# Four edits to the opening of a three-block transformer kernel: statistics by pairs of row tiles, half-block loads, one modulation block summed partly by TensorE, two weight tiles split by GpSimd

## The reference, cut to what matters

```python
c_act = jax.nn.silu(c)
mod = c_act @ ada_w[l] + ada_b[l]
shift, scale, gate = jnp.split(mod[:, None, :], 3, axis=-1)
u = _rmsnorm(h, norm_g[l]) * (1.0 + scale) + shift
proj = u @ w_in[l]                  # 1024 x 1024 times 1024 x 7168
```

## Time and profile before

| | |
|---|---|
| median of 3 runs | 2764.53 us |
| span of the profiled execution | 2763.9 us (the median is 0.6 us above it) |
| TensorE busy | 2689.4 us, 97% of the span |
| VectorE, ScalarE, GpSimd busy | 2086.6, 1069.2, 477.0 us |
| the chain that ended last, by engine | TensorE 80%, VectorE 14%, issue 2% |
| opening, until the last matmul's end | 66.9 us |
| next block's first matmul | starts at 67.8 us |

### The profile page before, as it was taken

The page is one execution under the profiler, slowest core; times in us unless marked ns, Lnnn a source line. Parts: engine busy times, 40 slices in busy tenths (PEclk is TensorE's granted clock), DMA queues, the critical chain, the costliest instruction groups (busy, mean ns, idle before and its releaser), DMA issues.

```text
span 2763.9 us, 33573 instructions
## 1 busy us (share of the span) xinstructions
PE 2689.4 (97%) x13192; PEld 2199.6 (80%) x13192; DVE 2086.6 (75%) x2796; ACT 1069.2 (39%) x1599; POOL 477.0 (17%) x254
## 2 busy tenths in 40 slices
PE   6999999999999999999999999999999999999998
PEld 5888888888888878778875678888887888888887
DVE  6999998873724663369998886688186988887978
ACT  5111112243413332245537751365232554555332
POOL 0000000000100002001210001354211656655000
PEclk8999999999999999999999999999999999999999
DMA  5312222224325452011101032100132222225431
GB/s 223 116 63 69 94 97 61 84 92 142 99 107 175 136 176 90 31 62 39 47 30 36 32 123 96 46 31 23 62 115 80 96 77 89 87 77 188 170 99 61
DMA packets 97710, 250.18 MB, mean 91 GB/s; under 512 B 7361, under 2 KB 34369, under 8 KB 96018
## 3 DMA queue, kind: packets, MB, share of 16 engines
q1 hardware_dynamic: 93010, 231.49, 24.4%
q10 hardware_dynamic: 4288, 15.73, 1.5%
q0 software_dynamic: 256, 0.82, 0.1%
HBM read 202.92 MB, written 45.09 MB: 90 GB/s over the span
## 4 chain that ended last, share of the span: by engine, by line
PE 80%; DVE 14%; issue 2%; ACT 1%; DMA 1%; DVEq 0%; ACTq 0%
PE pair L370 16%; PE pair L372 16%; PE pair L371 16%; PE pair L3657 7%; PE pair L3242 5%; PE pair L3244 5%; PE pair L3245 5%; DVE counted L1942 3%; PE pair L2593 2%; DVE reached L1993 1%; PE pair L2156 1%; DVE top_i L1999 1%; PE pair L1754 1%; PE pair L2172 1%; PE pair L2185 1%
## 5 line engine op out<-in xcount | busy, mean ns | idle before, releaser
L370 PE MATMUL pair<-u_hi,w_hi 128*128 128x512 f32 x768 | 302.1, 393 | 1.2 <-PEq L92 0.9
L641 DVE SCALAR_TENSOR_TENSOR conv_acc<-aT,cols,conv_acc 128x1024 f32<-128x1024 f32 x232 | 297.9, 1284 | 6.7
L371 PE MATMUL pair<-u_lo,w_hi 128*128 128x512 f32 x768 | 300.3, 391 | 0.0
L372 PE MATMUL pair<-u_hi,w_lo 128*128 128x512 f32 x768 | 300.3, 391 | 0.0
L370 PEld LDWEIGHTS pair<-u_hi,w_hi 128*128 128x128 f32 x768 | 145.2, 189 | 32.7 <-issue 2.4
L371 PEld LDWEIGHTS pair<-u_lo,w_hi 128*128 128x128 f32 x768 | 145.0, 189 | 30.6 <-issue 0.7
L372 PEld LDWEIGHTS pair<-u_hi,w_lo 128*128 128x128 f32 x768 | 145.0, 189 | 30.6
L370 PE MATMUL pair<-h_hi,ch_hi 128*128 128x512 f32 x392 | 153.8, 392 | 2.8 <-ACT ch L1824 2.6
L372 PE MATMUL pair<-h_hi,ch_lo 128*128 128x512 f32 x392 | 152.7, 389 | 0.0
L371 PE MATMUL pair<-h_lo,ch_hi 128*128 128x512 f32 x392 | 152.6, 389 | 0.0
L1014 POOL TENSOR_TENSOR yrT<-yrT,gate_c 128x1024 f32<-128x1024 f32 x8 | 18.9, 2366 | 758.1 <-ACT yrT L907 758.1
(11 more groups left out here) (510 smaller groups left out, 7105.1 us busy)
## 6 DMA issues: line engine op xcount, KB each, us to landing
wt<-in_w_ch SPq DMA_DIRECT2D x60, 512.0 KB, 3.4
wo_raw<-in_w_out SPq DMA_DIRECT2D x44, 512.0 KB, 3.6
wt<-in_w_up SPq DMA_DIRECT2D x10, 1024.0 KB, 4.9
w_raw<-in_w_up SPq DMA_DIRECT2D x10, 1024.0 KB, 4.8
g_spill<-g_stage SPq DMA_DIRECT2D x40, 256.0 KB, 2.2
ada_mod<-in_ada_mod SPq DMA_DIRECT2D x4, 2048.0 KB, 14.3
wt<-in_w_conv SPq DMA_DIRECT2D x16, 512.0 KB, 3.5
qk<-qk_st SPq DMA_DIRECT2D x8, 1024.0 KB, 6.4
```

What stands on the lines that cost most here:

```text
L370: nc.tensor.matmul(bank, w[0], x[0], start=(first and k == 0), stop=False)
L371: nc.tensor.matmul(bank, w[0], x[1], start=False, stop=False)
L372: return nc.tensor.matmul(bank, w[1], x[0], start=False, stop=(last and k == n_k - 1))
L641: nc.vector.scalar_tensor_tensor(dst, x, w, conv_acc[:], ALU.mult, ALU.add).then_inc(conv_step, 1)
```

## The change

- **Statistics by pairs.** `deviation` and the reciprocal (`inverse`) now serve two row tiles, four times; VectorE squares tiles 0, 1, 3, 5, ScalarE 2, 4, 6, 7. ScalarE's copy of tile 0 comes before its squares 6 and 7.
- **Half-block loads.** Each modulation block is loaded as two DMAs of 1 MB with a semaphore each. Block 2 has a place of its own and waits for nothing; block 3 waits for four transposed row tiles.
- **Shares of the sum.** VectorE sums slices 0 to 6 of block 0 (two of them before row tiles 6 and 7 are scaled), slices 6 and 7 of block 1, all 8 of block 2, slices 0 to 6 of block 3. For block 1 TensorE multiplies slices 0 to 5 as a streamed row: `cact` is the stationary operand of one column and the slice of 512 columns streams, six times, into one PSUM row; VectorE copies that row to `row_sb`, and TensorE turns it with four small matmuls.
- **GpSimd.** The high and low parts of weight tiles 0 and 1 are made by GpSimd (four instructions of 128 x 1024) and no longer by ScalarE and VectorE.
- **Order on TensorE and VectorE.** TensorE does the row sums and the step (0, 0) before the small matmuls of block 1, and the step (0, 4) before those of block 3. VectorE does `low(0)` before the sum of block 1, and waits for the row before `low(1)`.

```diff
+        ROW_SHARE = range(0, 6)
+        DVE_SHARE = (range(0, 7), range(6, KT), range(KT), range(0, 7))
+        mod_row = pair[3][0:1, 1, :]
@@ open_sync
-                sp.dma_start(ada_mod[j][:], a["ada_mod"][j, :, :].rearrange("p (k c) -> p k c", k=KT))\
-                    .then_inc(ada_in[j], 16)
+                src = a["ada_mod"][j, :, :].rearrange("p (k c) -> p k c", k=KT)
+                for half in range(2):
+                    ks = slice(half * KT // 2, (half + 1) * KT // 2)
+                    sp.dma_start(ada_mod[j][:, ks, :], src[:, ks, :]).then_inc(ada_in[j][half], 16)
...
-            sp.wait_ge(xt_mm, TT)
             modulation(2)
+            sp.wait_ge(xt_mm, 4)
             modulation(3)
@@ open_scalar
-            for half, tiles in enumerate(((0, 2), (4, 6, 7))):
-                for t in tiles:
-                    square(t)
-                deviation(half)
-            for t in range(TT):
...
-            high_part(act, 0)
+            deviation(0)
+            square(2)
+            deviation(1)
+            square(4)
+            deviation(2)
+            copy(0)
+            square(6)
+            square(7)
+            deviation(3)
+            for t in range(1, TT):
+                copy(t)
             act.wait_ge(xt_ok, TT)
-            modulated(0)
-            high_part(act, 1)
-            for k in range(1, KT):
+            for k in range(KT):
                 modulated(k)
             high_part(act, 2)
@@ open_vector
+            def modulation(j, first=0, upto=KT):
+                to = sum_dve[j][:]
+                dve.wait_ge(cact_ok, 1)
+                for done, k in list(enumerate(DVE_SHARE[j]))[first:upto]:
+                    dve.wait_ge(ada_in[j][k // 4], 16)
+                    x, c = ada_mod[j][:, k, :], cact[:, k:k + 1]
+                    if done == 0:
+                        nc.vector.tensor_scalar(to, x, c, None, ALU.mult).then_inc(step_dve[j], 1)
+                        continue
+                    dve.wait_ge(step_dve[j], done)
+                    nc.vector.scalar_tensor_tensor(to, x, c, to, ALU.mult, ALU.add).then_inc(step_dve[j], 1)
...
+            def weight_parts(n):
+                pool.wait_ge(glu_w[n], 16)
+                nc.gpsimd.tensor_tensor(w_parts[0][:, n, :, :], wt[:, n, :, :],
+                                        ones_col[:].rearrange("p (a b) -> p a b", b=1).broadcast_to([P, KT, P]),
+                                        ALU.mult).then_inc(job_hi, 1)
+                pool.wait_ge(job_hi, n + 1)
+                nc.gpsimd.tensor_tensor(w_parts[1][:, n, :, :], wt[:, n, :, :], w_parts[0][:, n, :, :].bitcast(F32),
+                                        ALU.subtract).then_inc(job_lo, 1)
@@ open_tensor
+            def row_sums():
+                for k in ROW_SHARE:
+                    pe.wait_ge(ada_in[1][k // 4], 16)
+                    last = nc.tensor.matmul(mod_row, cact[:, k:k + 1], ada_mod[1][:, k, :], start=(k == 0),
+                                            stop=(k == ROW_SHARE[-1]))
+                last.then_inc(row_mm1, 1)
...
             modulation(0)
-            for j in range(N_MOD):
...
+            row_sums()
+            tile_step(pe, 0, 0)
+            modulation(1)
+            tile_step(pe, 1, 0)
+            tile_step(pe, 0, 1)
+            tile_step(pe, 1, 1)
+            modulation(2)
+            for k in (2, 3, 4, 5):
+                for n in range(2):
+                    tile_step(pe, n, k)
+                    if k == 4 and n == 0:
+                        modulation(3)
```

More of the change, by code:

```diff
@@ L229, in open_vector @@
             chain = Count(dve, dve1)
-            steps = [0] * N_MOD
             def square(t):
@@ L235, in square, with inverse, normalize @@
                                                op0=ALU.mult, op1=ALU.add, accum_out=ss[:, t:t + 1]).then_inc(sq_dve, 1)
-            def normalize(half):
-                dve.wait_ge(std_done, half + 1)
-                r = rstd[:, 4 * half:4 * half + 4]
-                chain.then(nc.vector.reciprocal(r, r))
-                for t in range(4 * half, 4 * half + 4):
-                    dve.wait_ge(x_in[t // 2], 16)
-                    nc.vector.tensor_scalar(x_sb[:, t, :], x_sb[:, t, :], rstd[:, t:t + 1], None, ALU.mult).then_inc(xn_ok, 1)
-            def modulation(j, count):
-                dve.wait_ge(ada_in[j], 16)
-                for k in range(steps[j], steps[j] + count):
-                    x, c, to = ada_mod[j][:, k, :], cact[:, k:k + 1], ada_sum[j][:]
-                    if k == 0:
-                        nc.vector.tensor_scalar(to, x, c, None, ALU.mult).then_inc(ada_step, 1)
-                        continue
-                    dve.wait_ge(ada_step, N_SUM * j + k)
-                    nc.vector.scalar_tensor_tensor(to, x, c, to, ALU.mult, ALU.add).then_inc(ada_step, 1)
-                steps[j] += count
+            def inverse(q):
+                dve.wait_ge(std_done, q + 1)
+                r = rstd[:, 2 * q:2 * q + 2]
+                nc.vector.reciprocal(r, r).then_inc(inv_set, 1)
+            def normalize(t):
+                dve.wait_ge(inv_set, t // 2 + 1)
+                dve.wait_ge(x_in[t // 2], 16)
+                nc.vector.tensor_scalar(x_sb[:, t, :], x_sb[:, t, :], rstd[:, t:t + 1], None, ALU.mult).then_inc(xn_ok, 1)
             def shift_and_scale(j):
@@ L482, in _ @@
                 open_vector(dve)
+            @block.gpsimd
+            def _(pool):
+                open_gpsimd(pool)
         clear_semaphores(keep=[s for s in held if not any(s is o for o in opening)])
```

108 lines of the change are left out of this document (64 added, 44 removed).

## The result

| | before | after |
|---|---|---|
| median of 5 runs each | 2764.77 us (2764.33 to 2766.40) | 2775.23 us (2772.38 to 2778.10) |
| ratio to before | | 1.0038 [1.0027, 1.0048] |
| time and span of the profiled execution | span 2763.9 | 2773.05, span 2771.2 |
| TensorE, VectorE, GpSimd busy | 2689.4, 2086.6, 477.0 | 2695.8, 2083.3, 487.6 |
| last opening matmul ends | 66.9 | 72.7 |

The change costs 10.5 us, 0.38%; 2769.1 was forecast, with 2774.5 as the upper end. A second series of five gave 2775.01 (2772.56 to 2778.33), ratio 1.0035 [1.0023, 1.0048], and there the kernel before had 2765.88, so that the loss is 9.1 us. The profiled execution above is one of the shortest; the second series gave a trace of an execution of 2775.01, which stands for the median.

A forecast was written before the change was run, and what follows sets the result against it. TensorE was taken to bound the kernel, so opening delays carry to the end: 4.3 late plus 0.3 half clock on span 2763.9 gives 2768.5, plus 0.6 for the median: 2769.1 us, range 2762.0 to 2774.5.

The forecast's parts named there:

- The path: Opening followed by the four `g1` starts to TensorE's last opening matmul, forecast near 71.2 instead of 66.9, 4.3 late.
- the turns: Block 0's sum: VectorE additions and GpSimd splits alternate by whole instructions; three turns cost 5.2 us.
- The additions: VectorE's five chained additions of block 0, 1.8 to 2.8 us instead of 0.75 beside GpSimd, ending near 28.3.
- step (0, 4): TensorE step ahead of block 3's small matmuls, waiting for `low(4)` until about 57.3; new order costs 1.15 + 1.36.
- The row at full clock: Six float32 matmuls of 512 columns on TensorE for block 1: 5.2 us at full clock, 10.3 at half.
- GpSimd is truly hidden: Rival, block 0's sum: no turns, additions end at 23.1, opening 3.9 us early, 2760.6 us; chance 0.15.
- the row does not bring the clock up: Rival, block 1's row: clock stays 0.50, row takes 10.3, opening 9.7 late, 2774.3 us; chance 0.17.
- no loss of clock: Rival: full clock at 28.4, small matmuls 1.3 and row 2.1 less, 0.9 late, 2765.4 us; chance 0.10.
- the half clock may return in the idle pieces near 46 and 56: Late opening, TensorE: further half clock, mostly under other waits, added as 0.3 us.
- The forecast's own stretch at half clock: TensorE in block 0's small matmuls and the row's first 2.5 matmuls, at half clock until 35.7.
- the median lies 0.6 above its span: Whole kernel: 0.6 us added to the forecast span of 2768.5, giving 2769.1.
- four `g1`: VectorE's marks in the opening, forecast at 31.8, 42.2, 49.7 and 60.8, against 28.07, 36.79, 46.06 and 54.50 before.

The follow-up runs named there:

- the kernel with GpSimd late: Changed kernel, but GpSimd splits the weight tiles only after VectorE's sum of block 0 is complete; 2771.23 us, ratio 1.0019.
- with one wait: Changed kernel, with VectorE's additions waiting once for each half block instead of once for each slice; 2774.79 us, ratio 1.0032.
- the kernel before with GpSimd's splits: Kernel before, with only the splits of weight tiles 0 and 1 moved to GpSimd; 2774.03 us, ratio 1.0031.
- the version with sums ahead and no row: Kernel without GpSimd's splits, one wait per half block, sums of blocks 2 and 3 taken ahead, block 1 summed without the row; 2765.59 us, ratio 0.9996.
- without GpSimd: Changed kernel, with weight tiles 0 and 1 split by ScalarE and VectorE again, all else kept; 2765.41 us, ratio 1.0001.
- four copies: Changed kernel with splits back on ScalarE and VectorE, plus four unread plain GpSimd copies of the same tiles; 2769.40 us, ratio 1.0014.
- two instructions: Changed kernel with splits back on ScalarE and VectorE, plus GpSimd's first two split instructions, results unread; 2774.43 us, ratio 1.0026.
- with four: Changed kernel with splits back on ScalarE and VectorE, plus GpSimd's four split instructions, results unread; 2776.79 us, ratio 1.0033.
- the run that kept the clock up: Changed kernel with unread 512-column matmuls in three of TensorE's waits (4, 3 and 1); 2774.37 us, ratio 1.0027.
- the fastest version: Kernel without GpSimd's splits, one wait per half block, sums of blocks 2 and 3 ahead, row kept, one unread TensorE matmul; 2761.63 us, ratio 0.9984.

## Why the prediction was wrong

**What held.** The path and the turns. The additions ended at 28.38 (28.3), the first `g1` at 31.88 (31.8), the second at 42.48 (42.2), TensorE waited before step (0, 4) (until 58.51, where I had 57.3), and from the fourth `g1` to the end lay 10.6 us (10.4). The row at full clock takes 5.31 us (5.2), seen in the kernel with GpSimd late; in the changed kernel it ran from 31.51 to 38.12 (31.4 to 38.7) with the clock rising in it. These are the marks of the short execution. Of the rivals, "GpSimd is truly hidden" is refuted by the additions, "the row does not bring the clock up" by the row, and "no loss of clock" by the 0.50 from 24.1.

**The step that failed is one term of the sum**: "the half clock may return in the idle pieces near 46 and 56, mostly under other waits, for which I add 0.3". In the traced median execution it came back at 43.8 for 3.4 us and at 60.9 for 6.8, and TensorE was busy throughout both. The first of the two lay under a wait; the other stood on the path, in step (0, 4) and the small matmuls, and put the fourth `g1` back by another 1.9. The forecast's own stretch at half clock reached 37.0 where I had 35.7, so that the row took 8.07 (7.3) and the second `g1` came 1.3 later than in the short execution. All told this cost 3.3 us more than there (75.61 against 72.31), for a term of 0.3. One trace of before could not show this: before places its stretches alike in both its traces (27.1 and 27.0), the changed kernel does not (24.1 and 26.7). The Trainium skill (TensorE: Matmul & The Clock Gate, Part 1) says that one kernel sees a different number of slow matmuls from run to run. The two traces of the changed kernel agree (13.6 and 20.5 us at half clock), and it should have been a reason for a wider range.

**Smaller sizes.** In the short execution the opening was 5.8 longer, not 4.3. Its four `g1` and its end stand 0.1, 0.3, 0.8, 1.3 and 1.5 behind the forecast. Up to the second `g1` the small matmuls of block 1 took 39.70 to 42.11 = 2.4 instead of 1.7 (they start 0.31 apart where half of them have one row of `row_sb` as stationary operand), but the row ended 0.6 early, with a clock that rose 1.4 early. Behind it the additions cost most: 0.84 each instead of 0.78, for 13 of them on the path in blocks 2 and 3, 0.8 in all; 0.05 of each is the second wait (with one wait 5.55/7 = 0.79). And the time lies 1.7 to 1.9 above the span in nearly every execution (up to 2.2 in the kernel before with GpSimd's splits and in the version with sums ahead and no row). So "the median lies 0.6 above its span" compared a profiled execution with runs that were not it, and 1.8 belonged there.

Balance: 2763.9 + 4.3 + 1.5 (sizes) + 3.3 (clock) + 1.8 (time over span) = 2774.8, against 2775.2 measured and 2769.1 forecast. The 3.3 stand for the median execution by one trace of it. The executions of 2777 and more were not traced.

**Where it leads.** The turns were priced rightly, and half of the 6.1 us that were missed is half clock. GpSimd alone costs 8.2 us in the kernel before and 9.6 in the changed one, for additions that last 7.0 and 4.8 us longer. That the excess in the changed kernel is half clock behind the longer waits fits the traces (13.6 us of it in the opening without GpSimd, 20.5 with four copies, 23.9 with two instructions and with four), but is argued: the run that kept the clock up shortened the opening and not the median time.

## What to carry to other kernels

Work on GpSimd was not free for VectorE where both used operands in SBUF: count the additions that it will hold, and put it where VectorE does nothing or nothing that is waited for; a run of the same instructions whose results nobody reads shows the price. Allow for half clock behind a wait of TensorE, and where its place differs between executions take more than one trace before a term is set. A microsecond gained in the opening is not yet one in the median: look at where the two traces part again. Taking sums ahead of need was clearly faster than before only together with the row and one unread matmul; which of the three does it was not separated clear of noise.

## What the runs showed of the hardware

- **The turns decide waits late in the program as well.** In three of the 18 traces TensorE waits 2.0 us at 2543 to 2551 us, in the others not at all. The timeline there of one that does, the kernel without GpSimd's opening work (POOL, DVE, PE):

```profile
2536.61 2.39 POOL L3681 TENSOR_TENSOR dn_w_lo<-wa,dn_w_hi 128x1024 fp32r<-128x1024 f32 x1
...
2536.73 5.60 DVE L3544 TENSOR_TENSOR g_stage<-c_lin 128x512 f32<-128x512 f32 x2 [0.34 <-ACT c_lin L3402]
...
2538.96 2.83 POOL L3683 TENSOR_TENSOR dn_x_lo<-xa,dn_x_hi 128x1024 fp32r<-128x1024 f32 x1
...
2543.08 0.47 PE L3293 MATMUL pair<-h_hi,op_hi 128*128 128x512 f32 x1 [1.98 <-DVE c_raw L3524]
```

  Two instructions of a form that takes 0.68 us alone take 5.60 beside GpSimd's two (3.55 in the trace of the kernel before, also beside GpSimd), and TensorE waits for the VectorE instruction behind them. This is one source of the spread between executions; what decides it from one to the next was not tried.
- **The turn is not for two-input instructions only.** VectorE's TENSOR_SCALAR with one tile as input took 2.60 beside GpSimd (0.48 alone), and GpSimd's plain copy of 1.50 held additions too. The Trainium skill (SBUF — State Buffer, Who interferes with whom) names copies and TENSOR_SCALAR of VectorE among the instructions that can take the shared ports. The 2.60 agree for TENSOR_SCALAR; no run here shows a copy of VectorE held.
- **The clock can fall while TensorE is busy.** Stretches of the fastest version, columns as above:

```profile
20.00:24.90 4.90, 4.61 (x35) 3.71 (x34) 3.01 (x4) 4.35 (x5) 0.00 (x0) 1.00 1.03 436
24.90:28.30 3.40, 3.40 (x6) 0.48 (x6) 2.89 (x6) 2.76 (x3) 0.00 (x0) 0.51 1.01 427
28.30:52.20 23.90, 21.97 (x104) 15.61 (x102) 19.43 (x27) 12.10 (x11) 0.00 (x0) 1.00 0.41 171
```

  TensorE is busy for 4.61 of 4.90 us, with transposes, one matmul of 512 columns and small ones (its last longer idle time, 1.77, ended at 18.07), and then its clock falls to half for the first part of the row, in which it is busy throughout. It is back at 2.4 GHz from 28.3, with the row still streaming. In the changed kernel's median execution TensorE is busy for all of 37.00 to 43.80, from 40.97 to 43.4 in small matmuls, and half clock begins at 43.80.
